# Turning the mixer's output y: from TensorE's transposes to VectorE's 32x32 transposes with a trip through DRAM

## What is computed

```python
y = y + d_skip.astype(jnp.float32).reshape(G, R)[..., None] * xs
...
y = y * jax.nn.silu(z.astype(jnp.float32).reshape(bsz, L, G, R * P))
y = y * lax.rsqrt(jnp.mean(y * y, axis=-1, keepdims=True) + EPS)
y = y * ssm_norm_w.astype(jnp.float32).reshape(G, R * P)
...
y = jnp.concatenate([y_pool, y_ssm], axis=-1)
h = h + jnp.einsum('ble,ed->bld', y, w_out[i])
```

## Time and profile before

| | us |
|---|---|
| median of the timed runs | 2664.63 |
| lowest and highest | 2664.20, 2665.22 |
| the profiled execution | 2663.49 |
| its span | 2661.8 |

### The profile page before, as it was taken

The page is one execution under the profiler, slowest core; times in us unless marked ns, Lnnn a source line. Parts: engine busy times, 40 slices in busy tenths (PEclk is TensorE's granted clock), DMA queues, the critical chain, the costliest instruction groups (busy, mean ns, idle before and its releaser), DMA issues.

```text
span 2661.8 us, 37490 instructions
## 1 busy us (share of the span) xinstructions
PE 2642.3 (99%) x13962; PEld 2213.7 (83%) x13962; DVE 1661.3 (62%) x2228; ACT 1252.7 (47%) x2526; POOL 1092.2 (41%) x866
## 2 busy tenths in 40 slices
PE   8999999999999999999999999999999999999998
PEld 6888788888888888898888888888888888888887
DVE  6788615788157882377853576564445765666667
ACT  4667653666236672256634455554545222222223
POOL 2133440335003350033443688665655535353434
PEclk9999999999999999999999999999999999999999
DMA  9977666744558536575473655673436742423323
GB/s 335 303 259 244 240 243 248 241 175 179 216 184 262 189 146 248 202 211 209 167 269 135 225 190 208 249 266 131 173 132 226 295 145 103 164 95 127 119 95 158
DMA packets 278850, 532.70 MB, mean 200 GB/s; under 512 B 63994, under 2 KB 146942, under 8 KB 270606
## 3 DMA queue, kind: packets, MB, share of 16 engines
q1 hardware_dynamic: 278670, 530.31, 56.6%
HBM read 384.31 MB, written 145.95 MB: 199 GB/s over the span
## 4 chain that ended last, share of the span: by engine, by line
PE 96%; SPq 1%; DMA 1%; DVE 1%; issue 0%; ACT 0%; POOL 0%; POOLq 0%; ACTq 0%
PE bank L2260 23%; PE bank L2228 22%; PE bank L1849 21%; PE bank L1956 13%; PE bank L1936 8%; PE bank L2040 2%; PE bank L2002 1%; PE bank L2057 1%; PE bank L2020 1%; PE bank L2028 1%; DMA w_scr<-w_both 1%; PE bank L2008 1%; SPq L730 0%; PE bank L1968 0%; PE bank L2015 0%
## 5 line engine op out<-in xcount | busy, mean ns | idle before, releaser
L1849 PE MATMUL bank<-hnT_hi,w_ring 128*128 128x512 f32 x1152 | 367.0, 391 | 0.0
L2260 PE MATMUL bank<-w_first,T_hi 128*128 128x512 f32 x896 | 275.8, 389 | 0.0
L2390 DVE SCALAR_TENSOR_TENSOR acc<-pre,par,acc 128x512 f32<-128x512 f32 x240 | 211.4, 881 | 82.6 <-ACT pre L1365 76.8
L1849 PEld LDWEIGHTS bank<-hnT_hi,w_ring 128*128 128x128 f32 x1152 | 216.2, 188 | 44.7 <-ACT win_tmp L1494 0.5
L2756 DVE TENSOR_TENSOR acc_th<-bank,acc_th 128x512 f32<-128x512 f32 x224 | 150.0, 685 | 157.5 <-PE bank L2260 156.6
L2228 PE MATMUL bank<-T_hi,w_both 128*128 128x512 f32 x768 | 242.5, 389 | 0.5 <-DVE ff L2697 0.5
L1956 PE MATMUL bank<-w_ring,T_hi 128*128 128x512 f32 x768 | 239.0, 392 | 0.0
L1849 PE MATMUL bank<-hnT_lo,w_ring 128*128 128x512 f32 x576 | 224.4, 390 | 0.0
L2260 PEld LDWEIGHTS bank<-w_first,T_hi 128*128 128x128 f32 x896 | 168.2, 188 | 34.9
L1936 PE MATMUL bank<-w_ring,hnT_hi 128*128 128x384 f32 x768 | 195.8, 335 | 1.3 <-DMA w_ring<-w_scr 1.3
L1849 PE MATMUL bank<-hnT_hi,w_both 128*128 128x512 f32 x544 | 182.0, 406 | 0.9 <-ACT pre L1365 0.9
(11 more groups left out here) (316 smaller groups left out, 6255.4 us busy)
## 6 DMA issues: line engine op xcount, KB each, us to landing
w_ring<-w_scr SPq DMA_DIRECT2D x312, 512.0 KB, 4.3
T_scr<-stage SPq DMA_DIRECT2D x32, 1792.0 KB, 6.7
w_scr<-w_both SPq DMA_DIRECT2D x100, 512.0 KB, 4.2
pair_raw<-in_w_ff SPq DMA_DIRECT2D x36, 1024.0 KB, 5.5
third<-T_scr SPq DMA_DIRECT2D x28, 1024.0 KB, 4.9
pair_raw<-T_scr SPq DMA_DIRECT2D x28, 1024.0 KB, 4.8
sums<-sums_scr SPq DMA_DIRECT2D x64, 384.0 KB, 4.9
raw<-in_w_in SPq DMA_DIRECT2D x36, 512.0 KB, 6.5
```

The source lines that it names most:

```text
L1849: mm = nc.tensor.matmul(bank[s][:, :], w[:, k, :], t[:, k, :], start=(k == 0 and j == 0), stop=(k == KT - 1 and j == 2))
L2260: mm = nc.tensor.matmul(bank[4 * half + t][:, :], a[:, k, tok], w[:, k, :], start=(SECOND[q % 7] not in GOES_ON and k == 0 and j == 0), st ...
L2390: ins = nc.vector.scalar_tensor_tensor(acc[:, s, 0:TB], pre[:, s, k:k + TB], w, acc[:, s, 0:TB], ALU.mult, ALU.add)
```

## The change

y of a step is turned by VectorE and not by TensorE. y_turning(q) transposes 128 tokens by 384 features in 32x32 blocks from y into y_turn, which lies on the group's place in T_hi, in step q+2 as before (the last two behind the mixer). That turns each block but leaves the blocks in their place. For each group, SP writes the three tiles of all four chunks to DRAM in one DMA (store_y, 0.79 MB, 512-byte runs) and reads them back in four (load_y), each with 32 partitions of 1536 pieces of 128 bytes, into y_raw, which lies in the group's place of T_lo; there each block stands where a full transpose would have put it. Then one y_high and one y_low work on 128x1536 elements each, in place of four of 128x384, y_low of group 0 in step 9, of group 1 in step 13, of group 2 and 3 behind the mixer; y_high of group 2 in u=0 and of group 3 in u=2 (block 0: u=3) on ScalarE. Store and loads of groups 0 and 1 stand between the units of the input product; those of groups 2 and 3 between the weights of the output product. TensorE waits for the low parts at units 0, 3 and 6, and SP's wait before quad's loads is now for the last low part. ScalarE's y_high no longer waits for the turned h's store to free T_hi; y_turning does, on VectorE. The semaphores and the scratch in DRAM are left out below.

```diff
--- before.py
+++ after.py
@@ -248,6 +248,8 @@
...
         ffn_w = at("ffn_w", [P, D_MODEL], xdt_at)
+        y_turn = at("y_turn", [P, 3 * GROUPS, CH, P], T_hi_at + 4 * 2048)
+        y_raw = at("y_raw", [P, 3 * GROUPS, TB], T_lo_at + 4 * 2048)
         h_junk = at("h_junk", [P, D_MODEL], T_lo_at + 14 * 2048)
@@ -380,9 +383,11 @@
...
         yn_ready = sig("yn_ready", STEPS)
-        yT_ps = sig("yT_ps", STEPS)
-        yT_hi = sig("yT_hi", STEPS)
-        yT_lo = sig("yT_lo", STEPS)
+        y_turned = sig("y_turned", STEPS)
+        y_stored = sig("y_stored_then_split_loaded", 16 * GROUPS, 0)
+        y_back = sig("y_back_then_split_loaded", 64 * GROUPS, 0)
+        yT_hi = sig("yT_hi", GROUPS)
+        yT_lo = sig("yT_lo", GROUPS)
         pool_hi = sig("pool_hi", 4)
@@ -819,6 +824,22 @@
...
+                def store_y(b, g):
+
+                    y_turned.wait(sp, b, CH * (g + 1))
+                    sp.dma_start(y_scr[b, g].rearrange("i c p f -> p (i c) f"),
+                                 y_turn[:, 3 * g:3 * g + 3, :, :].rearrange("p i c f -> p (i c) f")
+                                 ).then_inc(y_stored.sem, 16)
+
+                def load_y(b, g):
+
+                    y_stored.wait(sp, b, 16 * (g + 1))
+                    blocks = y_scr[b, g].rearrange("i c (s a) (j f) -> j a (i c s) f", a=32, f=32)
+                    for j in range(4):
+                        sp.dma_start(y_raw[32 * j:32 * j + 32, 3 * g:3 * g + 3, :].rearrange(
+                            "p i (c f) -> p (i c) f", f=32), blocks[j]
+                            ).then_inc(y_back.sem, 16)
+
                 def load_quarter(i):
@@ -863,11 +884,25 @@
...
                                 store_turned_h(b - 1, t)
+                        if b and n in (3 * UNITS_G, 4 * UNITS_G):
+                            store_y(b, n // UNITS_G - 3)
+                            load_y(b, n // UNITS_G - 3)
+                        if b == 0 and n in (26, 34):
+                            store_y(b, (n - 26) // 8)
+                        if b == 0 and n in (28, 35):
+                            load_y(b, (n - 28) // 7)
                     for d in range(2):
...
                                        ].rearrange("(k p) c -> p k c", p=P))
+                            if (d, i) == ((0, 2) if b else (0, 3)):
+                                store_y(b, 2)
+                                load_y(b, 2)
+                            if (d, i) == ((0, 5) if b else (0, 6)):
+                                store_y(b, 3)
+                            if (d, i) == ((0, 6) if b else (0, 7)):
+                                load_y(b, 3)
                             if b < LAST and (d, i) == (0, 3):
@@ -879,7 +914,7 @@
...
-                                yT_ps.wait(sp, b, STEPS)
+                                yT_lo.wait(sp, b, GROUPS)
                                 up_out.wait(sp, b, ups(b))
@@ -1429,13 +1464,9 @@
...
-                def y_high(b, q):
-                    g, c = divmod(q, CH)
-                    yT_ps.wait(act, b, q + 1)
-                    if b and q == CH:
-                        hT_stored.wait(act, b - 1, 64 * CH)
-                    nc.scalar.activation(T_hi[:, 4 + 3 * g:7 + 3 * g, c * P:(c + 1) * P],
-                                         bank[2][:, 0:GW].rearrange("p (i t) -> p i t", t=P),
+                def y_high(b, g):
+                    y_back.wait(act, b, 64 * (g + 1))
+                    nc.scalar.activation(T_hi[:, 4 + 3 * g:7 + 3 * g, :], y_raw[:, 3 * g:3 * g + 3, :],
                                          ACT.Copy).then_inc(yT_hi.sem, 1)
@@ -1571,8 +1602,8 @@
...
                             y_squares(b, q - 1)
-                        if q > 1:
-                            y_high(b, q - 2)
+                        if q in (9, 13):
+                            y_high(b, q // CH - 2)
                         tanh(b, n1)
@@ -1594,7 +1625,6 @@
...
                     y_squares(b, STEPS - 1)
-                    y_high(b, STEPS - 2)
@@ -1604,13 +1634,14 @@
...
                                 y_norm(b, STEPS - 1)
+                                y_high(b, 2)
                             if d == 0 and u in (1, 2):
...
                                                          ACT.Copy).then_inc(pool_hi.sem, 1)
-                            if d == 0 and u == 2:
-                                y_high(b, STEPS - 1)
+                            if (d, u) == ((0, 2) if b else (0, 3)):
+                                y_high(b, 3)
                             if b == LAST:
@@ -2021,14 +2052,6 @@
...
-                def y_transposes(b, q):
-                    yn_ready.wait(pe, b, q + 1)
-                    yT_lo.wait(pe, b, q)
-                    for i in range(3):
-                        mm = nc.tensor.transpose(bank[2][:, i * P:(i + 1) * P],
-                                                 y[:, i * P:(i + 1) * P], ident[:, :])
-                    mm.then_inc(yT_ps.sem, 1)
-
                 def diagonal(b, q):
@@ -2130,8 +2153,6 @@
...
                             unit(b, n1)
-                        if q > 1:
-                            y_transposes(b, q - 2)
                         if q:
@@ -2143,7 +2164,6 @@
...
                         y_offset(b, q, g, c)
-                    y_transposes(b, STEPS - 2)
                     diagonal(b, STEPS - 1)
@@ -2175,8 +2195,8 @@
...
                                 pool_lo.wait(pe, b, 4)
-                            if d == 0 and u == 6:
-                                yT_lo.wait(pe, b, STEPS)
+                            if d == 0 and u in (0, 3, 6):
+                                yT_lo.wait(pe, b, 2 + u // 3)
                             if d == 0:
@@ -2184,8 +2204,6 @@
...
                                 fold(N + 3)
-                            if d == 0 and u == 2:
-                                y_transposes(b, STEPS - 1)
                             if b < LAST and (d, u) == (0, 7):
@@ -2459,11 +2479,21 @@
...
+                def y_turning(b, q):
+
+                    g, c = divmod(q, CH)
+                    yn_ready.wait(dve, b, q + 1)
+                    if b and q == CH:
+                        hT_stored.wait(dve, b - 1, 64 * CH)
+                    nc.vector.transpose(y_turn[:, 3 * g:3 * g + 3, c, :],
+                                        y[:, :].rearrange("p (i f) -> p i f", f=P)
+                                        ).then_inc(y_turned.sem, 1)
+
                 def y_finish(b, q):
...
                     ty_ready.wait(dve, b, q + 1)
-                    yT_ps.wait(dve, b, q)
+                    y_turned.wait(dve, b, q)
                     ssy_ready.wait(dve, b, q)
@@ -2491,12 +2521,10 @@
...
-                def y_low(b, q):
-                    g, c = divmod(q, CH)
-                    yT_hi.wait(dve, b, q + 1)
-                    tiles = (slice(None), slice(4 + 3 * g, 7 + 3 * g), slice(c * P, (c + 1) * P))
-                    nc.vector.tensor_tensor(T_lo[tiles],
-                                            bank[2][:, 0:GW].rearrange("p (i t) -> p i t", t=P),
+                def y_low(b, g):
+                    yT_hi.wait(dve, b, g + 1)
+                    tiles = (slice(None), slice(4 + 3 * g, 7 + 3 * g), slice(None))
+                    nc.vector.tensor_tensor(T_lo[tiles], y_raw[:, 3 * g:3 * g + 3, :],
                                             T_hi[tiles].bitcast(F32), ALU.subtract
@@ -2570,6 +2598,8 @@
...
                             masked = mask()
+                        if q > 1:
+                            y_turning(b, q - 2)
                         if q:
@@ -2596,13 +2626,9 @@
...
                                                 per_head(dtt, c, g), ALU.mult)
-                        if b == 0 and n1 is None:
-                            y_low(b, q - 2)
                         nc.vector.tensor_tensor(by_head(xw[:, :]), by_head(xb[:, :]),
...
                                                 ).then_inc(xw_ready.sem, 1)
-                        if q > 1 and (b or n1 is not None):
-                            y_low(b, q - 2)
                         if b:
@@ -2616,6 +2642,8 @@
...
                             finish(b, pending - 1)
+                        if q in (9, 13):
+                            y_low(b, q // CH - 2)
                         if b == 0 and q < STEPS - 1:
@@ -2624,19 +2652,21 @@
...
                         pending = n2[-1]
+                    y_turning(b, STEPS - 2)
                     y_finish(b, STEPS - 1)
...
                     state_add(b, STEPS - 1)
-                    y_low(b, STEPS - 2)
                     finish(b, pending - 1)
                     finish(b, pending)
+                    y_turning(b, STEPS - 1)
+                    y_low(b, 2)
                     for i in range(4):
...
                                                 ).then_inc(pool_lo.sem, 1)
-                    y_low(b, STEPS - 1)
+                    y_low(b, 3)
...
```

## The result

| | before | changed |
|---|---|---|
| median of the timed runs, us | 2664.41 | 2695.30 |
| lowest and highest | 2663.35, 2665.22 | 2692.50, 2697.59 |
| the profiled execution | 2663.49 | 2696.68 |
| its span | 2661.8 | 2695.0 |

The ratio is 1.0116, with a 95% interval of 1.0098 to 1.0133. The forecast was 2668, and the measured time lies 13 us above its range. The time of the changed kernel also spreads more, over 5.1 us where the kernel before has 1.9.

A forecast was written before the change was run, and what follows sets the result against it. TensorE, busy 99% and 96% of the chain, was taken as the bound. 2663.5 - 21.8 + 0.7 + 4.4 + 9.6 + 8.3 + 3.0 = 2667.7 us, forecast 2668, no measurable change; range 2649 to 2682.

The forecast's parts named there:

- The removed transposes: TensorE: 64 groups of three transposes removed, each worth 0.34 us, 21.8 us gained.
- The DVE terms: VectorE in the mixer: transpose and low part cancel per step; 0.7 us lost once in block 0, 4.4 at mixers' ends.
- Group 3, last block: Output product: SP waits for the last y_low before quad's loads, unit 7's weights queue behind; stall 9.6 us (5.5 to 14).
- The price of a group's loads: DMA queue: 6144 pieces of 128 bytes take about 5.5 us, with ends of 2.1 and 10 us.
- the rival of a collapse: 128-byte reads at a tenth of 147 GB/s: 53 us a group, about 2.86 ms in all; chance 0.02.
- Group 3, block 0: Output product: store delays unit 5 by 2.1 us, ScalarE's wait for the loads stalls unit 6 by 6.2; 8.3 together.
- Group 3, blocks 1 and 2: Output product: x's load also queued, landing some 2 us later against unit 6; stall 1.5 us each, 3.0 together.
- The clock: TensorE: granted clock 1.00 (2.4 GHz) in every window quoted; the sum had no term for a lower clock.
- the late landing: Rival: group 3's last four loads land 3 us later, costing all four blocks, 12 us together, 2680 us; chance 0.23.

The follow-up runs named there:

- the two edits above: Against the changed kernel: VectorE's transposes moved behind yo of their own step, 2695.58 us; low part of group 1 moved behind the mixer's last gate and state, 2695.16 us.
- the two runs whose edits act only in the last block: Against the changed kernel: quad's four loads one behind each of units 7 to 10, 2680.06 us; SP's wait before quad put back to y turned, 2688.99 us.

## Why the prediction was wrong

**The removed transposes: right.** 0.34 us a group was predicted and 0.30 to 0.36, mostly 0.33, shows at the steps that have nothing else in them. The 390 ns of the Trainium skill (VectorE: DVE Perf Modes, "The three transpose paths") for each transpose, given there for bf16, which the prediction set aside, would have been wrong by a factor of 3.5: three fp32 ones in the stream cost 0.34.

**The DVE terms: the step that failed.** I had written that per step the transpose and the low part it replaces cancel, and took 0.7 + 4.4 us; it was 16.9. Their lengths do nearly cancel (0.57 and 0.545 us). Their places don't. VectorE's timeline before, in one of the last steps (start us, us, line, idle in brackets):

```profile
1330.75 0.55 DVE L2601 TENSOR_TENSOR xw<-xb,dte 128x384 f32<-128x384 f32 x1
1331.22 0.54 DVE L2498 TENSOR_TENSOR T_lo<-bank,T_hi 128x384 fp32r<-128x384 f32 x1
1331.88 1.03 DVE L2490 TENSOR_TENSOR xw_both<-xw,xw_both 128x384 fp32r<-128x384 f32 x1
```

and in the changed kernel:

```profile
1348.54 0.55 DVE L2629 TENSOR_TENSOR xw<-xb,dte 128x384 f32<-128x384 f32 x1
1349.68 1.03 DVE L2520 TENSOR_TENSOR xw_both<-xw,xw_both 128x384 fp32r<-128x384 f32 x1 [0.59 <-ACT xw_both L1479]
...
1353.49 0.56 DVE L2488 STREAM_TRANSPOSE y_turn<-y 128x384 f32<-128x384 f32 x1
1354.24 0.56 DVE L2505 TENSOR_TENSOR y<-bank,ty 128x384 f32<-128x384 f32 x1 [0.19 <-issue]
```

The low part stood where VectorE waits for ScalarE's high part of xw, and was free; now that gap is idle. The transpose stands ahead of the gate, and the gate, which waits for its end, starts 0.75 us after the transpose did. In the last steps VectorE sets TensorE's pace, so all of it shows. The long low part of group 1, 1.9 us in step 13, comes on top. Putting group 3 back on TensorE removed most of the loss (0.75 us of 3.3 stay), and in that kernel the low part stands in the gap again:

```profile
642.49 0.55 DVE L2661 TENSOR_TENSOR xw<-xb,dte 128x384 f32<-128x384 f32 x1
642.96 0.54 DVE L2549 TENSOR_TENSOR T_lo<-bank,T_hi 128x384 fp32r<-128x384 f32 x1
643.63 1.02 DVE L2541 TENSOR_TENSOR xw_both<-xw,xw_both 128x384 fp32r<-128x384 f32 x1
```

The prediction read the last gate and missed what leads up to it. Blocks 1 to 3 also lose 0.9 us in step 10 each, where I had looked at block 0 alone: y_low of group 0 delays the state, and the run with it moved to step 11 shows that step without the loss. Of block 0's 4.8 us the two edits above took away 2.2; the place of the rest is not shown.

**Group 3, last block: the mechanism right, the size short.** Low part against unit 6: 0.3 us early predicted, 0.4 late measured. From quad's issue to unit 7's weights 15.3 was predicted and 16.8 measured. The wait ahead of unit 7 was put at 9.6 and was 11.0, with 2.5 of slow clock behind it. The price of a group's loads was put at 5.5 us of queue. (Each of the four loads has 1536 pieces in all, 48 for each of its 32 partitions.) Here is the window that holds nearly nothing else (us, us; busy of PE, PEld, DVE, ACT, POOL; clock, DMA share, GB/s) beside the one ahead of it:

```profile
1380.00:1386.00 6.00, 6.00 (x28) 4.99 (x27) 0.00 (x0) 0.00 (x0) 0.00 (x0) 1.00 1.04 367
1386.00:1392.00 6.00, 6.00 (x29) 4.95 (x28) 0.00 (x0) 0.00 (x0) 0.00 (x0) 1.00 1.06 126
```

It moved 126 GB/s in 128-byte pieces, by which 0.79 MB take 6.3 us; the written pieces of the turned h gave 147 at a share of 0.88. The window has a lull in it, 54 GB/s from 1388 to 1389: SP issued the fourth load only at 1388.34. In the run with quad's wait put back, where it was issued at 1383.92, the stretch from 1384 to 1388 has no lull and moved 131 to 145 GB/s, by which they take 5.7. So the price was near what was predicted; from first issue to last landing the four took 7.9 us. The factor to the unbroken transfers ahead of them is 2.9, so the rival of a collapse fell. The Trainium skill (DMA: Bandwidth & Descriptors, "Specifications") wants 512 bytes or more for the full rate, and the trace agrees in direction, 126 against 367 GB/s.

**Group 3, block 0: right.** Unit 5 was to wait 2.1 and unit 6 6.2 us; the table has 2.14 (2.18 less the 0.04 of unit 4) and 6.22. y's loads were put at 339.5 and ScalarE's high part started at 340.12. What is missing is 1.9 us of slow clock. That unit 6 was late through ScalarE's order is right only in part: with y_high behind high_part, high_part waited for the stores of split weights until 340.5, and the order was worth 1.3 us.

**Group 3, blocks 1 and 2: too low.** 1.5 us each was predicted, 3.8 and 2.3 measured, and 1.6 and 1.7 of slow clock. The run with h behind the loads shows that without h's 2.1 MB ahead they fit, with x where it was.

**The clock: left out.** Four of the five waits of over 2 us ahead of a unit were followed by matmuls at the lower of TensorE's two levels. Windows around the longest wait (the same columns) and TensorE's timeline behind it:

```profile
1402.00:1412.00 10.00, 0.00 (x0) 0.00 (x0) 2.36 (x2) 1.59 (x2) 7.20 (x3) 0.59 1.04 398
1412.00:1414.00 2.00, 1.40 (x3) 1.17 (x4) 0.00 (x0) 0.00 (x0) 2.00 (x2) 0.50 1.02 406
1414.00:1416.00 2.00, 2.00 (x6) 1.58 (x5) 0.43 (x1) 1.54 (x2) 1.92 (x2) 0.50 1.04 414
1416.00:1418.00 2.00, 2.00 (x7) 1.54 (x7) 0.35 (x2) 2.00 (x3) 2.00 (x2) 0.63 1.02 406
1418.00:1420.00 2.00, 2.00 (x10) 1.64 (x9) 1.30 (x2) 1.07 (x2) 1.26 (x1) 1.00 0.51 205
```

```profile
1412.60 1.22 PE L1987 MATMUL bank<-w_ring,T_hi 128*128 128x512 f32 x2 [11.02 <-DMA w_ring<-w_scr]
1413.62 0.63 PE L1987 MATMUL bank<-w_ring,T_lo 128*128 128x512 f32 x1
...
1419.11 0.62 PE L1987 MATMUL bank<-w_ring,T_hi 128*128 128x512 f32 x2
1419.57 0.40 PE L1987 MATMUL bank<-w_ring,T_lo 128*128 128x512 f32 x1
```

The granted clock stood at 1.00 up to the wait and at 0.50 (1.2 GHz) when the work came back, and a matmul took 0.63 in place of 0.40 us for some 5 us: 2.5 us lost on top of 11. The four places make 7.7 us (1.9, 1.6, 1.7 and 2.5 from block 0 to 3), and these, counted as busy, are half of what keeps TensorE's busy time from falling by 21.5 us (it fell by 5.4). The Trainium skill (TensorE: Matmul & The Clock Gate, Part 1) tells of the same two levels, slow after idleness; the trace agrees. It was there to be added to the stalls of the sum. The length of a wait alone does not tell it. Ahead of unit 5 of block 0 TensorE waited 2.1 us and the clock stayed at 1.00 (first line); in the run with ScalarE's other order it waited 2.2 us at the same place and the clock fell (second line):

```profile
338.00:340.00 2.00, 2.00 (x11) 1.65 (x10) 0.00 (x0) 0.00 (x0) 0.00 (x0) 1.00 1.24 267
338.00:340.00 2.00, 2.00 (x6) 1.54 (x5) 0.00 (x0) 0.00 (x0) 0.00 (x0) 0.50 0.98 319
```

**The sum again.** 2667.7, with 11.8 more for VectorE, 7.7 for the clock, 3.1 for blocks 1 and 2, 1.4 and 0.6 for the last block's units 7 and 6, 2.2 for the start of block 1, 1.5 ahead of the first step, and 0.3 less gained by the groups: 2696.3, where the profiled execution took 2696.7. Of the rivals none was it: the late landing alone was to cost the four output products; the largest error lay on an engine that the prediction had called balanced. What delays the start of block 1 stays open. It is no fixed cost of the change: in the two runs whose edits act only in the last block it was 0.6 and 0.4 us, and without the trip 0.0. With group 3 on TensorE it was 1.7 to 3.1 in all four profiles, and no run says why.

## What to carry to other kernels

Exchanging two instructions of equal length on an engine costs nothing only if both stand in the same wait: look at what is idle beside the one that goes, and what waits for the one that comes. A trip through DRAM is cheap while it is covered by a whole step and dear where its last data is also the first that is needed; keep the short path for the last group and the trip for the others. And a stall ahead of TensorE behind which its clock falls costs its length and, here, 1.6 to 2.5 us more.

## What was not expected of the hardware

VectorE's transpose of 128x384 fp32 took 0.57 us, 0.1 more than its rate on 1024 columns gave (0.47), and the next instruction that waits for it began 0.19 later. Moving h behind y's loads (2.1 MB, 5.5 us of queue) was worth 14.4 us by the medians (13.1 by the traces, without the scatter), where each VectorE edit alone moved the time by nothing that can be told. And 126 GB/s at a share of 1.06 beside 367 at 1.04 means that a DMA share that looks full does not say how much is moved.
